# Both heads in one step: the 64-wide attentions with 64-row scores and one step for all compressed keys

## The reference, cut to what matters

```python
s = q @ k.T * scale + mask          # 512 queries, blocks of 128
p = exp(s - max(s)); l = sum(p)     # by row
o = (p @ v) / l                     # 64 wide
# last attention: o = g0*o_cmp + g1*o_slc + g2*o_win
```

## Time and profile before

| | us |
|---|---|
| median of 3 runs | 2417.02 (2410.09 to 2423.25) |
| the profiled execution, its own time | 2415.6 |
| its span | 2413.8 |
| 40 slices, TensorE's granted clock | 0.8 to 1.0 of full speed |
| `amem`, first scores to first output product | 344.4 to 371.4 |
| `bq` with its ramp | 839.6 to 961.0 |
| `bmem` | 961.0 to 986.2 |
| `nq` with its ramp and tail | 2035.9 to 2354.0 |

### The profile page before, as it was taken

How to read it: one execution, slowest core, us unless ns; L and a number is a source line. 1 busy time by engine, 2 the same in 40 slices (tenths; PEclk the granted TensorE clock), 3 DMA queues, 4 the chain that set the end, 5 groups by cost and what they waited for, 6 DMA issues and landing times.

```text
span 2413.8 us, 34422 instructions
## 1 busy us (share of the span) xinstructions
PE 2273.4 (94%) x10882; PEld 1855.7 (77%) x10882; DVE 1298.2 (54%) x2537; ACT 921.1 (38%) x1850; POOL 250.7 (10%) x143
## 2 busy tenths in 40 slices
PE   7986999999999799999999999999999689999997
PEld 6675777888888687788888888888887667777766
DVE  5876444666644566466664454555544643545443
ACT  4433453322322266432223332222223334555551
POOL 0042221000001111110000210000002000011112
PEclk8998999999999999999999999999999889999888
DMA  3121111332333110223232332222222312000001
GB/s 131 51 88 53 61 53 62 96 101 90 104 102 102 66 36 26 77 90 99 93 104 96 104 97 96 99 99 96 96 96 79 113 63 85 2 19 9 19 10 70
DMA packets 50053, 182.93 MB, mean 76 GB/s; under 512 B 5552, under 2 KB 5680, under 8 KB 49840
## 3 DMA queue, kind: packets, MB, share of 16 engines
q1 hardware_dynamic: 49824, 181.35, 22.9%
q0 software_dynamic: 144, 0.52, 0.1%
HBM read 179.76 MB, written 2.10 MB: 75 GB/s over the span
## 4 chain that ended last, share of the span: by engine, by line
PE 83%; DVE 7%; issue 4%; ACT 3%; POOL 1%; DMA 1%; DVEq 0%; ACTq 0%; POOLq 0%; SPq 0%
PE pj L1863 68%; PE ps L2006 4%; PE po L2062 4%; PE pt L2022 2%; ACT w_hi L670 1%; DMA raw<-in_wstream 1%; PE po L2047 1%; PE ps L2176 1%; DVE s_sb L1303 1%; PE pj L1973 1%; DVE rtmp L1248 1%; DVE w_lo L1118 1%; PE po L2071 1%; ACT p_sb L757 1%; DVE rtmp L1245 1%
## 5 line engine op out<-in xcount | busy, mean ns | idle before, releaser
L1863 PE MATMUL pj<-h_hi,w_hi 128*128 128x512 f32 x1736 | 706.9, 407 | 21.0 <-DVE w_lo L1118 15.6
L670 ACT ACTIVATE w_hi<-raw 128x1024 fp32r<-128x1024 f32 x334 | 353.7, 1059 | 865.6 <-PE pj L1863 848.8
L1863 PE MATMUL pj<-h_lo,w_hi 128*128 128x512 f32 x1736 | 683.8, 394 | 0.0
L1863 PE MATMUL pj<-h_hi,w_lo 128*128 128x512 f32 x1736 | 683.6, 394 | 0.0
L1118 DVE TENSOR_TENSOR w_lo<-raw,w_hi 128x1024 fp32r<-128x1024 f32 x288 | 390.4, 1356 | 392.2 <-ACT w_hi L670 391.9
L1863 PEld LDWEIGHTS pj<-h_hi,w_hi 128*128 128x128 f32 x1736 | 331.1, 191 | 90.1 <-issue 17.1
L1863 PEld LDWEIGHTS pj<-h_hi,w_lo 128*128 128x128 f32 x1736 | 330.5, 190 | 71.1
L1863 PEld LDWEIGHTS pj<-h_lo,w_hi 128*128 128x128 f32 x1736 | 331.5, 191 | 64.6 <-issue 1.4
L1863 PE MATMUL pj<-G_hi,w_hi 128*128 128x512 f32 x704 | 278.1, 395 | 3.1 <-DVE G_lo L1367 3.0
L1863 PE MATMUL pj<-G_lo,w_hi 128*128 128x512 f32 x704 | 276.0, 392 | 0.0
L1863 PE MATMUL pj<-G_hi,w_lo 128*128 128x512 f32 x704 | 275.9, 392 | 0.0
(11 more groups left out here) (295 smaller groups left out, 2531.4 us busy)
## 6 DMA issues: line engine op xcount, KB each, us to landing
raw<-in_wstream SPq DMA_DIRECT2D x334, 512.0 KB, 3.4
xT<-in_x SPq DMA_DIRECT2D x4, 512.0 KB, 9.5
out_x<-xT SPq DMA_DIRECT2D x4, 512.0 KB, 2.7
memT<-in_mem SPq DMA_DIRECT2D x1, 1024.0 KB, 12.3
cst<-in_cst SPq DMA_DIRECT2D x1, 512.0 KB, 10.5
tab<-in_tab POOLq DMA_DIRECT2D x1, 512.0 KB, 5.0
posi<-in_pos SPq DMA_DIRECT2D x1, 256.0 KB, 2.8
vec<-in_vec SPq DMA_DIRECT2D x1, 182.5 KB, 2.4
```

Of the source, the lines that this page charges most:

```text
L670: nc.scalar.activation(w_hi[:, c.par * CW:(c.par + 1) * CW], raw[:, c.par * CW:(c.par + 1) * CW], ACT.Copy).then_inc(hi_ready, 1)
L1863: mm = nc.tensor.matmul(acc, w[:, col:col + P], x[part], start=first and k == 0, stop=last and k == 2)
```

## The change

The unit of the 64-wide attentions becomes a step of both heads of a pair. A new class `Pairs` stands beside `Attention` (which stays for the 128-wide one), with a planner of its own on each engine.

- Keys are no longer padded. A head's score matmul takes only its own 64 partitions of the queries and of the keys: head 0 rows 0 to 63, head 1 rows 64 to 127, one behind the other, into two PSUM banks.
- A step is one query block of a branch for both heads: 4 steps per tile in the band and memory attentions, 9 in `nq`, because all of `cmp` is one step: four 32-column score matmuls per head side by side in a bank, one mask addition per head, one reduction for the maxima of all eight (head, block) pairs, one subtraction, one exponential of 256 columns without row sum (a reduction makes it in `scale_pass`), two full transposes, one copy, and one values matmul of 256 columns per head against values that are laid out block-diagonally (`cmp_v`, zero elsewhere).
- Up to 256 columns, both heads' transposed blocks go to one bank and are copied by one ACT instruction; wider ones by two.
- TensorE's order is scores of step k+1, transposes of k, values of k-1, and in it the projection pieces. TensorE's tiles are written out in full and no longer looped. Semaphores count steps (`pair_turned`, `pair_valued`) or step-and-head.
- The transposes of step k wait for the copies of k-1. ScalarE's exponentials of step k+1, of both heads, wait for the transposes of step k. The turned probabilities get a second buffer for alternate steps.
- GpSimd's zero fills of `b_k` (128x4096) and of `n_k` (twice 128x4096) are gone; `cmp_v` (128x1024) is filled instead. `mem_k` is one copy where it was two, `cmp_k` too; `cmp_v` takes five ACT instructions where it took two.

```diff
+class Pairs:
+    def __init__(self, name, tiles, branches, first_step, first_tile, first_pass, out0):
+        self.steps = [(branch, b) for branch in branches for b in (range(1) if branch == "cmp" else range(NB))]
...
+        self.at_rope = {"bq": 1, "nq": 4}.get(name)
+        self.at_refill = {"bq": 1, "nq": 7}.get(name, 3)
...
-            pool.wait_ge(x_ready, RESIDUALS["down0"] + DT)
-            nc.gpsimd.memset(b_k[:, :], 0.0).then_inc(zeroed, 1)
...
-            nc.gpsimd.memset(n_k["win"][:, :], 0.0)
-            nc.gpsimd.memset(n_k["slc"][:, :], 0.0).then_inc(zeroed, 1)
+            nc.gpsimd.memset(cmp_v[:, :], 0.0).then_inc(zeroed, 1)
...
+            def pair_softmax(ph, i, j, k):
...
+                act.wait_ge(pair_turned, s)
+                if branch == "cmp":
+                    act.wait_ge(pair_max, s * 2 + 2)
+                    nc.scalar.activation(pc[:, :], s_sb[:, 0:2 * P], ACT.Exp, scale=ph.scale).then_inc(pair_exp, 2)
+                    return
+                for hh in range(2):
+                    act.wait_ge(pair_max, s * 2 + (hh + 1))
...
+            def pair_bring(ph, i, j, k):
+                act.wait_ge(pair_turned, s + 1)
+                if w <= MEM:
+                    nc.scalar.activation(dst[:, 0:2 * w], pt[0][:, 0:2 * w], ACT.Copy).then_inc(pair_copied, 2)
+                    return
+                for hh in range(2):
+                    nc.scalar.activation(dst[:, hh * S:hh * S + w], pt[hh][:, 0:w], ACT.Copy).then_inc(pair_copied, 1)
+
+            def pair_tile(ph, i, j):
+                for k in range(ph.n):
+                    pair_softmax(ph, i, j, k + 1)
+                    pair_bring(ph, i, j, k)
+                    if k == 2 and not (isinstance(i, int) and j == 0):
+                        output_hi(ph, i, j - 1)
...
+            def pair_maximum(ph, i, j, k):
+                if branch == "cmp":
+                    dve.wait_ge(pair_scored, s * 2 + 2)
+                    dve.wait_ge(pair_exp, s * 2)
+                    for hh in range(2):
+                        nc.vector.tensor_tensor(s_sb[:, hh * P:(hh + 1) * P], ps[hh][:, 0:P], C("cmp", 0, P),
+                                                ALU.add).then_inc(pair_taken, 1)
+                    link(nc.vector.tensor_reduce(cmx[:, :], each, mybir.AxisListType.X, ALU.max))
+                    nc.vector.tensor_tensor(each, each, cmx[:, :].unsqueeze(2).broadcast_to([P, 8, NCMP]),
+                                            ALU.subtract).then_inc(pair_max, 2)
...
+            def pair_scores(ph, t, k):
+                    pe.wait_ge(pair_taken, 2 * s)
+                for hh in range(2):
+                    rows = slice(hh * 64, hh * 64 + 64)
+                    if branch == "cmp":
+                        for c in range(NB):
+                            mm = nc.tensor.matmul(ps[hh][:, c * NCMP:(c + 1) * NCMP],
+                                                  qn[rows, par * S + c * P:par * S + (c + 1) * P],
+                                                  cmp_k[rows, g * NCMP:(g + 1) * NCMP], start=True, stop=True)
+                    else:
...
+                        mm = nc.tensor.matmul(ps[hh][:, 0:w], q[rows, par * S + b * P:par * S + (b + 1) * P], keys,
+                                              start=True, stop=True)
+                    mm.then_inc(pair_scored, 1)
+
+            def pair_turn(ph, t, k):
+                    pe.wait_ge(pair_copied, 2 * s)
+                for hh in range(2):
+                    pe.wait_ge(pair_exp, 2 * s + hh + 1)
...
+            def pair_tile(ph, t):
+                for k in range(ph.n):
+                    pair_scores(ph, t, k + 1)
+                    if ph.name == "bq":
+                        query(ph, 0, t + 2, range(2 * k, 2 * k + 1))
+                    pair_turn(ph, t, k)
+                    if k:
+                        pair_values(ph, t, k - 1)
+                    elif t:
+                        pair_values(ph, t - 1, ph.n - 1)
+                    if k == 1 and t:
+                        turn_output(ph, 0, t - 1)
+                    if ph.name == "bq":
+                        query(ph, 0, t + 2, range(2 * k + 1, 2 * k + 2))
+                    if ph.name == "nq" and t < ph.tiles - 2 and k < CB:
+                        query(ph, 0, t + 2, range(k, k + 1))
```

More of the change, by code:

```diff
@@ L161, in _attentions @@
         score, unit, tile, done = score + n, unit + n, tile + tiles, done + tiles * len(branches)
+    step = 0
+    for name, tiles, branches, out0 in (("amem", 2, ["mem"], 8), ("bq", 8, ["band"], 0), ("bmem", 2, ["mem"], 8),
+                                        ("nq", 8, ["cmp", "slc", "win"], 0)):
+        made[name] = Pairs(name, tiles, branches, step, tile, done, out0)
+        step, tile, done = step + tiles * made[name].n, tile + tiles, done + tiles * len(branches)
     return made
@@ L968, in _ @@
                     if k < 2:
-                        act.wait_ge(chunk_used, c.v + 3)
-                        for hh in range(2):
-                            last = nc.scalar.activation(mem_k[l][:, (2 * k + hh) * MEM:(2 * k + hh + 1) * MEM],
-                                                        pj[t.par][:, 0:MEM], ACT.Copy, scale=V("half", hh))
-                        last.then_inc(pj_free[t.par], 1)
+                        take(mem_k[l][:, k * MEM:(k + 1) * MEM], t, c, n=MEM)
                     else:
@@ L1387, in _, with attention @@
-            LINKS = {"aq": 2 * (2 + 1), "amem": 0, "bq": 2 * (2 + 2), "bmem": 0, "nq": 2 * (2 + 6)}
-            def attention(name, begun=False):
-                ph = ATT[name]
-                if name == "amem":
+                    if last and v == ph.at_lo:
+                        output_lo(ph, *last[:2])
+            def attention(ph):
+                maximum(ph, 0, 0, 0)
+                maximum(ph, 0, 0, 1)
+                attention_tiles(dve, ph, tile, link, 2 * (2 + 1))
+                end = ph.tiles - 1
+                scale_pass(ph, 0, end, 0)
+                output_lo(ph, 0, end)
@@ new lines, in pair_tile @@
+            def pair_tile(ph, i, j):
+                first = isinstance(i, int) and j == 0
+                for k in range(ph.n):
+                    pair_maximum(ph, i, j, k + 1)
+                    if k == 0 and not first:
+                        scale_pass(ph, i, j - 1, ph.passes - 1)
+                    if k - 1 in ph.ends[:-1]:
+                        scale_pass(ph, i, j, ph.ends.index(k - 1))
+                    if k == 1 and ph.name == "nq" and not first:
+                        gate_output(ph, i, j - 1)
+                    if k == 3 and ph.name != "nq" and not first:
+                        output_lo(ph, i, j - 1)
+                    if more(ph, i, j) and ph.at_rope is not None and k in (ph.at_rope, ph.at_rope + 1):
+                        query(ph, i, j + 1, k - ph.at_rope)
+                    if k == ph.n - 1 and ph.name == "nq" and ahead(ph, i, j):
+                        take_query(ph, i, j + 2)
@@ L1392, in attention, with pair_attention @@
+            def pair_attention(ph):
+                if ph.name == "amem":
                     have_factor("mem")
-                if name == "nq":
+                if ph.name == "nq":
                     dve.wait_ge(silu_ready, CT + dict(STAGES)["nz"])
                     take_query(ph, 0, 0)
-                for part in range(0 if begun else 2):
+                for part in range(2 if ph.at_rope is not None else 0):
                     query(ph, 0, 0, part)
-                if name == "nq":
+                if ph.name == "nq":
@@ new lines, in pair_turn @@
+            def pair_turn(ph, t, k):
+                branch, b = ph.steps[k]
+                s = step_of(ph, 0, t, k)
+                w = ph.keys(k)[1]
+                if s:
+                    pe.wait_ge(pair_copied, 2 * s)
+                else:
+                    pe.wait_ge(pT_ready, ATT["aq"].first_unit + ATT["aq"].tiles * ATT["aq"].n + 2)
+                for hh in range(2):
+                    pe.wait_ge(pair_exp, 2 * s + hh + 1)
+                    src = pc[:, hh * P:(hh + 1) * P] if branch == "cmp" else p_sb[:, hh * S:hh * S + w]
+                    dst = pt[0][:, hh * w:(hh + 1) * w] if w <= MEM else pt[hh][:, 0:w]
+                    for kb in range(w // P):
+                        mm = nc.tensor.transpose(dst[:, kb * P:(kb + 1) * P], src[:, kb * P:(kb + 1) * P], ident)
+                mm.then_inc(pair_turned, 1)
@@ L2106, in attention, with pair_attention @@
+            def pair_attention(ph):
+                if ph.name in ("bq", "nq"):
+                    for j in range(2):
+                        query(ph, 0, j)
+                pair_scores(ph, 0, 0)
+                for t in range(ph.tiles):
+                    pair_tile(ph, t)
+                pair_values(ph, ph.tiles - 1, ph.n - 1)
                 turn_output(ph, 0, ph.tiles - 1)
@@ L2300, in _ @@
             mm.then_inc(chunk_used, 1)
[L2301 removed]
```

(1 more changed line is left out.)

407 lines of the change are left out of this document (247 added, 160 removed).

## The result

The changed kernel takes 2426.9 us (median of 20 runs, 2417.2 to 2433.6) where the kernel before takes 2417.5: ratio 1.0036, 95% interval 1.0026 to 1.0047. It is slower by 9 us; the forecast was 31 less. The result lies outside of the range. By the yardstick of half a per cent that the prediction used this is no change; the interval of the 20 runs leaves out 1 all the same.

What follows compares the result with a forecast made beforehand. TensorE, busy 94% of the span, was taken as the bound. Terms of -25 (last attention's tiles), -10 (clock), +2 (banded), +5 (memory) and -3 (zero fill) sum to -31 us, forecast 2385, range 2352 to 2415.

Steps and rivals of the forecast that it cites:

- Projections, refills of the weight chunks and their DMAs move by parts of a step only; GpSimd [...] keeps its cover.: Last attention (`nq`): these moves cost nothing, with GpSimd busy only 6.2 us of a 36.1 us tile.
- Memory attentions: `amem` and `bmem`: +5 us together, +2 over 16 steps and +3 ahead of the first transposes of four phases.
- the low clock spreads to the other attentions: Attentions other than the last: a named sign that the forecast is wrong, with no size given.
- ScalarE's round takes over, so faster scores buy nothing: Memory attentions: a round of 2.3 us exceeds TensorE's 2.2 us for two units; +2 us over 16 steps.
- Front of `bq`: Ahead of the banded attention: dropping GpSimd's zero fill frees VectorE, and so the values TensorE waits for; -3 us.
- `nq` without the collision: Last attention: -25 us from eight tiles, each 3.1 shorter, and -10 us from a higher clock.
- The compressed step: Each tile of the last attention: TensorE needs 2.6 us where eight compressed units took 5.7, saving 3.1.
- rival 2: Last and banded attentions: fuller overlap of the heads' scores, or the whole clock, giving 2352 to 2375 us; chance 0.13.
- The shape: TensorE's row-shape change around half-row scores: 0.25 us per step, adding 2.3 per tile of the last attention.
- my -10: Last attention: half of some 20 us lost to the low clock comes back; -10 us, bounds 0 to -20.
- `bq` without the collision: Banded attention: per tile -0.8 us for scores and +1.0 for shape changes; +2 us in eight tiles.
- rival 3: Last attention: ScalarE's round exceeds TensorE's step by 0.9 us in 72 steps, +65, 2450 us; decides from 0.43; chance 0.10.

Runs made afterwards that it cites:

- e1: changed kernel with the weight-chunk refill moved, in `bq` from step 1 to 2 and in `nq` from 7 to 5; 2390.5 us, ratio 0.9883.
- e5: e1 with memory attention keys padded with zeros to 128 rows again; 2367.9 us, ratio 0.9805.
- e9: e5 with GpSimd's zero fill put back in front of `bq`, as two fills with VectorE waiting for them; 2374.4 us in one run.
- e6: e1 with scores over all 128 rows in all four attentions, the two heads summed; 2374.3 us, ratio 0.9828.
- e10: e5 with the rotation of the next queries one step earlier in `nq`; 2358.3 us, ratio 0.9761.
- one filler: changed kernel with one extra 512-column matmul, its result unread, in each step of the memory attentions; 2415.6 us, ratio 0.9981.

## Why the prediction was wrong

In profiled spans the forecast was -31 and the result +8.9. Term by term:

- **The collision, not in the sum at all: +40** (24.0 in `nq`, 15.9 in `bq`, by e1, with what the clock adds behind the waits). This is the step that failed: "Projections, refills of the weight chunks and their DMAs move by parts of a step only; GpSimd [...] keeps its cover." GpSimd kept its cover, VectorE lost its own. The trace of before showed it: L1248's 1.58 us beside a remainder in `bq` was not looked at, and the earlier trace rows, where GpSimd's fill stretches another kind of VectorE instruction, was read as a peculiarity of the fill. The Trainium skill (SBUF — State Buffer, Who interferes with whom) has the rule: a VectorE instruction with two SBUF inputs contends with a GpSimd instruction that reads SBUF, and the one that starts second is blocked until the first has ended. The trace agrees: GpSimd's ends at 925.86 and L1354, whose own length is 0.69, at 926.41, 0.55 us later. L1437, which reads PSUM, keeps its length: at 256 columns 0.42 us in the 12 that start while GpSimd works on SBUF tensors and 0.42 in the 100 others.
- **Memory attentions: forecast +5, measured +19.7.** With 128 rows (e5) it is +2.4 and +2.8, so the term for ScalarE's round and the ramp was right within the 2 us that such a stage varies by, and the clock under half rows, 14.5 us, was missing. The prediction named "the low clock spreads to the other attentions" as what would make it wrong, but gave it no price: the step was "ScalarE's round takes over, so faster scores buy nothing", where the half rows took the clock away.
- **Front of `bq`: forecast -3, measured about +1.** "VectorE then works on to the values that TensorE waits 6.33 us for" skipped VectorE's wait for the factor. e9 shows it.
- **`nq` without the collision: forecast -35, measured -47.2** (e1). The tile was forecast at 33.0 and is 33.2, by two misses that cancel: TensorE's busy time fell by 5.3 (35.17 to 29.85) and not by 3.1, and its idle time rose by 2.4, from 0.9 to 3.3, where I counted nothing. The compressed step cost what was said: 1.48 scores, 0.27 transposes, 0.87 values and the shape's 0.10, 2.7 for 2.6. The scores overlap wholly, as rival 2 had it: passes 1 and 2 start together and so do 3 and 4, where the forecast had only the middle two side by side. The shape costs 0.30 for my 0.25. Yet all that the half rows brought in `nq` is 4 us (e6). The rest is the clock with the ramp and the tail: stage less eight tiles was 27 us and is 4 in e1 (269.0 less 8 x 33.1), -23 for my -10. The stage's clock went from 0.90 to 0.98.
- **`bq` without the collision: forecast +2, measured -3.2**. The kernel before's own collision is -4.4 of it, so +1.2 like for like.

The differences, 39.9 + 14.7 + 4 - 12.2 - 5.2, with -1.3 from stretches that are the same in both kernels, make the 39.9 between -31 and +8.9.

Of the rivals, rival 3 was the one of this sign, with another place: TensorE does wait more, by 2.4 us a tile in e1, but it decides only from 3.9 (nine steps by 0.43), and 1.1 of the 2.4 was VectorE's collision again (e10). The wait that decided was VectorE's, and hung on the step at which a third engine works. That the tile came out within 0.2 us of the forecast was luck.

The Trainium skill (TensorE: Matmul & The Clock Gate, Part 3) has matmuls in different row groups start about 4 ns apart. The overlap here agrees with it: two passes both start at 2210.46, and both heads take 0.43 us at 256 columns, without the 0.20 for the change of shape. The Trainium skill (TensorEngine Tiling (Array Packing), Key Properties) says that TensorE drains when the tiling mode changes, without a price. The trace agrees, with the 0.30 us above.

What stays open: why one filler was enough in `bmem` and not in `amem`, and why half rows keep the clock low there and not in the last two tiles of `nq` (e1); how much of the 23 us in `nq` is clock and not ramp or tail, and how much of it belongs to the compressed units alone, since no run changed only these; and how the two heads' passes come to start in pairs, though the kernel issues one head's matmul behind the other's.

## What to carry to other kernels

When work is moved in time, list for each step what GpSimd and VectorE will do at once. Here a VectorE instruction with both inputs in SBUF that met GpSimd's remainder lasted until 0.55 us behind its end, and moving the refill to another step was worth 36 us (2426.9 to 2390.5). Look for lengths that differ between like instructions in the trace of before, since they show which meetings are already there.

Packing two 64-row matmuls halved their time for 0.3 us per visit, but of the 2.0 us a tile that TensorE saved, 1.4 came back as waits. Read the granted clock of each stage that gets half rows, above all where no projections stand between its steps: with padded rows the two memory stages took 29.4 and 27.9 us, with half rows 38.2 and 37.6.

## What the runs showed of the hardware

- Half-filled rows and the clock: the memory stages with 64-row scores ran at 0.52 to 0.65 (at 0.50 over a stretch in which TensorE was busy 23.17 of 23.90 us), with 128 rows at 0.90 to 1.00, and three extra full-height matmuls per step brought 0.88 and 0.94.
- Two float32 matmuls on rows 0 to 63 and 64 to 127 took half the time of two on 128 rows (0.43 for 0.87 us at 256 columns), though each is two passes and one matmul is issued behind the other. The change of shape cost 0.10 us ahead of the first pass, 0.10 behind it and 0.10 behind the last.
- A GpSimd remainder of 2.35 us turned VectorE's 0.69 into 2.40 and 1.58, and a 256-column subtraction of 0.43 into 2.05. VectorE instructions that read PSUM kept their length beside it.
